# Second attention mixes two query tiles per pass, its result stored turned and normed in the projection, with stores and gate weights moved across stages

## What is computed

```python
attn = mla_attention(...)      # 4 heads of 128 value columns, causal softmax over 2048 keys
lru  = rg_lru_branch(...)      # 512 columns
mixed = concat([rms_norm(attn, attn_out_norm), rms_norm(lru, lru_out_norm)])
x  = x + gate1 * (mixed @ w_out)
h2 = rms_norm(x, norm2_g) * (1 + scale2) + shift2
x  = x + gate2 * hierarchical_moe(h2, ...)    # 32 experts, 2 for each row
```

## Time and profile before

| | us |
|---|---|
| median of 3 runs | 4110.98 (4110.75 to 4111.8) |
| the profiled execution, its own time | 4112.5 |
| span of its instructions | 4110.2 |
| busy in the span: TensorE, VectorE, ScalarE, POOL | 3780.2, 1954.9, 1557.4, 545.3 |

### The profile page before, as it was taken

One profiled execution on the slowest core, in us unless ns is written; L12 is line 12 of the kernel. 1 busy time (PEld: TensorE's weight loads), 2 busy tenths in 40 slices (PEclk: granted clock), 3 DMA queues, 4 the chain that ended last, 5 costly groups with the idle time before them and its releaser, 6 DMA issues. The chain is left out here.

```text
span 4110.2 us, 63078 instructions
## 1 busy us (share of the span) xinstructions
PE 3780.2 (92%) x21816; PEld 2452.9 (60%) x21834; DVE 1954.9 (48%) x4191; ACT 1557.4 (38%) x3427; POOL 545.3 (13%) x748
## 2 busy tenths in 40 slices
PE   6999999799889976999999799996999899599998
PEld 4667666555674534777777677773666555344444
DVE  1344333566575552111111278876333344678886
ACT  1122212356553431111111266664333222267675
POOL 0000000100260000111111001101000000322222
PEclk8999999899999988999999899997999999699999
DMA  6221121222524476656656212215221133488974
GB/s 237 77 89 70 68 97 56 86 85 79 162 87 177 163 275 249 209 171 206 203 164 217 69 49 66 67 37 151 62 89 45 42 124 125 179 292 297 318 244 102
DMA packets 228193, 573.83 MB, mean 140 GB/s; under 512 B 28170, under 2 KB 103051, under 8 KB 212159
## 3 DMA queue, kind: packets, MB, share of 16 engines
q1 hardware_dynamic: 178782, 395.92, 27.5%
q0 software_dynamic: 49248, 175.79, 14.5%
HBM read 433.59 MB, written 137.93 MB: 139 GB/s over the span
## 5 line engine op out<-in xcount | busy, mean ns | idle before, releaser
L2177 PE MATMUL out_psO<-out_w,out_mixT 128*128 128x512 f32 x1024 | 451.8, 600 | 3.0 <-ACT out_mixT L2148 1.6
L880 PE MATMUL inp_psU<-inp_w,inp_hT 128*128 128x512 f32 (+3 forms) x1376 | 420.8, 464 | 0.0
L880 PEld LDWEIGHTS inp_psU<-inp_w,inp_hT 128*128 128x128 f32 x1376 | 256.4, 190 | 152.3 <-issue 122.3
L2177 PEld LDWEIGHTS out_psO<-out_w,out_mixT 128*128 128x128 f32 x1024 | 194.0, 192 | 236.6 <-issue 236.5
L4200 DVE COPY moe_bu<-moe_wu 128x1024 f32 x480 | 299.1, 697 | 40.4 <-issue 18.2
L4087 PE MATMUL moe_psU<-moe_wu,moe_xT 128*32 x1280 | 293.4, 383 | 1.7 <-DVE moe_bu L4200 1.7
L4087 PE MATMUL moe_psU<-moe_bu,moe_xT 128*32 128x256 f32 x3840 | 294.5, 383 | 0.0
L876 PE MATMUL inp_psU<-inp_hT,inp_w 128*128 128x256 f32 x1088 | 244.4, 385 | 9.0 <-DVE inp_tm L682 4.5
L2721 PE MATMUL moe_psG<-moe_xT,moe_g_w 128*128 128x256 f32 x1024 | 234.3, 383 | 10.9 <-DMA moe_u_w<-in_w_up 10.9
L2762 ACT ACTIVATE moe_sg<-moe_psG 128x256 f32<-128x256 f32 x64 | 24.5, 383 | 577.6 <-PE moe_psG L2721 577.6
L2782 DVE TENSOR_TENSOR moe_hT<-moe_sg,moe_psG 128x256 f32<-128x256 f32 x64 | 26.9, 421 | 443.5 <-ACT moe_sg L2762 443.5
(11 more groups left out here) (687 smaller groups left out, 6700.6 us busy)
## 6 DMA issues: line engine op xcount, KB each, us to landing
moe_wu<-in_w_up SPq DMA_DIRECT2D x32, 2048.0 KB, 9.5
moe_d_w<-in_w_down SPq DMA_DIRECT2D x16, 2048.0 KB, 10.5
moe_wd<-in_w_down SPq DMA_DIRECT2D x32, 1024.0 KB, 11.3
moe_g_w<-in_w_gate SPq DMA_DIRECT2D x15, 2048.0 KB, 8.6
moe_u_w<-in_w_up SPq DMA_DIRECT2D x15, 2048.0 KB, 13.5
mod_w<-in_w_ada SPq DMA_DIRECT2D x24, 1024.0 KB, 14.1
inp_mod_w<-in_w_mod SPq DMA_DIRECT2D x16, 1024.0 KB, 4.9
xn<-out_xn POOLq DMA_DIRECT2D x32, 512.0 KB, 3.8
```

What stands on the lines that cost most here:

```text
L880: mm = pe.matmul(psU[:, u % NB, 0:n], hT[:, par, k, j * P:(j + 1) * P], w[:, k, lo:lo + n], start=(k == 0), stop=(k == KD - 1))
L2177: mm = pe.matmul(psO[:, j, h, :], mixT[:, j, k, :], out_weights.half[k // 4][:, k % 4, h * BANK:(h + 1) * BANK], start=(k == 0), stop=(k = ...
```

## The change

- In the second attention, two neighbouring query tiles (0 and 1, 2 and 3, ...) form a pair. `mix` now has a value block stationary and the probabilities of both tiles moving, 256 columns, and sums into one PSUM tile of 256 columns; a key block that only the odd tile sees moves 128 columns. So the result is made turned (value columns by queries). `pT` now holds all key blocks of a pair, once for long and once for short tiles. Which parts are mixed in which unit is worked out ahead (`mixed_by`); at most units one part (two key blocks), after the unit's `turn`.
- The engine that copies the unit's probabilities also copies a finished pair from PSUM to `o`. The reciprocals of the sums (`invert`) go by POOL to DRAM as one row of 256 numbers, and back spread over 128 partitions; VectorE multiplies `o` by them (`divide`), and POOL stores the pair turned.
- The second projection norms the turned attention: squares, a sum over four blocks, one matmul by ones that sums over the partitions and spreads the sum (`sum_squares`, between the two halves of `product`), square root on ScalarE, reciprocal and four products on VectorE. The four transposes and the copy are gone in block 2.
- In both projections the half of tiles 0 and 1 that needs no norm is multiplied first (`direct_part`). SP's first loads are in a new order, and x, gate row and router weights come last.
- The window attention, the recurrence and the second attention no longer wait for their last stores; the projection's SP does, before it reads them (`LeavingRows`).
- In `choose_rows` SP loads expert 0's gate weights and stores the chosen rows ahead of the modulation. In `experts` only halves of up are loaded for expert 0, the gate row comes after expert 0's loads, and POOL's first gather waits for the first half of up.
- The first half of the output weights, the turned input of the second projection and two buffers of the second experts move into one shared buffer with these gate weights.

```diff
 class SharedRows:
+        self.weights = nc.alloc_sbuf_tensor("shared_weights", [P, 4 * D], F32)
+        self.gate_landed = nc.alloc_semaphore("first_expert_gate_landed")
+    def load_gate(self, sp, w_gate):
+        sp.dma_start(self.weights_of(KD, FF1), w_gate[0:1, :, :].rearrange("e (k p) n -> p (e k) n", p=P)).then_inc(self.gate_landed, 16)
...
 def mlstm (and window_attention, latent_attention):
-            for x in range(2):
-                pool.wait_ge(stored[x], 16 * (NC - SKIP))
...
 def out_projection, sync:
-                rows.load_first(sp, 0)
+                direct_rows.all_stored(sp)
+                rows.load_direct(sp, 0, 0)
+                mix_rows.all_stored(sp)
+                rows.load_mix(sp, 0, 0)
+                rows.load_direct(sp, 1, 1)
+                sp.dma_start(nw[:, :], rows.norm_w.to_broadcast([P, 512])).then_inc(nw_landed, 16)
+                rows.load_mix(sp, 1, 1)
             out_weights.load_rest(sp)
-                rows.load_first(sp, 1)
+                for t in range(2):
+                    rows.load_x(sp, t, t)
...
 vector:
+            def norm_turned(t, j):
+                ch.done(dve.tensor_tensor(sq[:, 0:512], hv, hv, ALU.mult))
+                dve.tensor_reduce(sqs[:, :], sq[:, 0:512].rearrange("p (k t) -> p t k", k=4), AX, ALU.add).then_inc(msq, 1)
+                dve.wait_ge(rooted, t + 1)
+                ch.done(dve.reciprocal(root[:, :], root[:, :]))
+                for k in range(4):
+                    ins = dve.scalar_tensor_tensor(out=mixT[:, j, k, :], in0=mix[:, j, k * P:(k + 1) * P], scalar=nw[:, k:k + 1],
+                                                   in1=root[:, :], op0=ALU.mult, op1=ALU.mult)
...
 tensor:
+            def direct_part(t):
+                for h in range(2):
+                    for k in range(rows.direct, rows.direct + 4):
+                        pe.matmul(psO[:, t, h, :], mixT[:, t, k, :], out_weights.half[k // 4][:, k % 4, h * BANK:(h + 1) * BANK],
+                                  start=(k == rows.direct), stop=False)
...
+                ks = range(normed, normed + 4) if early(t) else range(KD)
                 for h in range(2):
+                    if h and layer == 2 and there(t + 1):
+                        sum_squares(t + 1)
+                    for k in ks:
...
+            def sum_squares(t):
+                pe.wait_ge(msq, t + 1)
+                pe.matmul(psM[:, 0:P], K["ones"][:, :], sqs[:, :], start=True, stop=True).then_inc(turned, 1)
...
 def choose_rows, sync:
-            mod.put(sp)
+            shared.load_gate(sp, w_gate)
             sp.wait_ge(rows_ready, 1)
...
+            mod.put(sp)
...
 def latent_attention, tensor:
-                for c in range(4 * g, min(4 * g + 4, tile_of[n] + 1)):
-                    mm = pe.matmul(psO[:, n % 2, :], pT[:, u % 2, c % 4, :], v[h % 2][:, c, :],
-                                   start=(c == 0), stop=(c == tile_of[n]))
+                    if x:
+                        pe.wait_ge(*out_count(x - 1))
+                pe.wait_ge(*kept_count(n, q // 2))
+                for c in (2 * q, 2 * q + 1):
+                    if c <= top:
+                        mm = pe.matmul(psO[:, :], v[h % 2][:, c, :], pT[k][:, c, :, :].rearrange("p x t -> p (x t)"),
+                                       start=(c == 0), stop=False)
+                    else:
+                        mm = pe.matmul(psO[:, P:2 * P], v[h % 2][:, c, :], pT[k][:, c, 1, :], start=False, stop=True)
...
 keep:
+            if parts_before(n, g):
+                wait(mixed, parts_before(n, g))
...
+            for x in range(NP):
+                if last_unit[x] == u:
+                    wait(mixed, first_part[x + 1])
+                    if x >= 2:
+                        wait(*stored_count(x - 2))
+                    copy(o[:, x % 2, :], psO[:, :]).then_inc(out_kept[keeper[x]], 1)
...
 vector:
+            def divide(x):
+                dve.wait_ge(*out_count(x))
+                dve.wait_ge(rb_landed, 16 * (x + 1))
+                dve.tensor_tensor(o[:, x % 2, :], o[:, x % 2, :], rb[:, x % 2, :], ALU.mult).then_inc(o_ready, 1)
...
 gpsimd:
+            for x in range(NP):
+                pool.wait_ge(rch, ends[x] + 1)
+                pool.dma_start(r_rows[x:x + 1, :].rearrange("a (j p) -> p (a j)", p=P), rc[:, x % 4, :], allow_slow_non_contiguous=True
+                               ).then_inc(r_stored, 16)
+                pool.wait_ge(r_stored, 16 * (x + 1))
+                pool.dma_start(rb[:, x % 2, :], r_rows[x:x + 1, :].to_broadcast([P, 2 * P])).then_inc(rb_landed, 16)
+                if x:
+                    put(x - 1)
```

More of the change, by code:

```diff
@@ L1038, in load_first, with __init__, all_stored @@
             sp.dma_start(self.wr[:, :, :], self.w_router).then_inc(self.wr_landed, 16)
+class LeavingRows:
+    def __init__(self, nc, stack, name, width, stores):
+        self.tile = stack.enter_context(nc.sbuf_tensor(f"{name}_o", [P, 2, width], F32))
+        self.stored = [nc.alloc_semaphore(f"{name}_stored{j}") for j in range(2)]
+        self.ALL = 16 * stores
+    def all_stored(self, engine):
+        for j in range(2):
+            engine.wait_ge(self.stored[j], self.ALL)
 class SharedRows:
@@ L1196, in _ @@
             blocks(pool, put)
-            for j in range(2):
-                pool.wait_ge(stored[j], 16 * (NBLK // 2))
         @block.tensor
@@ L2219, in body @@
                     product(n + 1, 1 - j)
-                if there(n + 2):
+                if there(n + 2) and layer == 1:
                     turn(n + 2, j)
@@ L2227, in body @@
                     route(n - 1)
+            for t in range(2):
+                direct_part(t)
+                if t == 0 and layer == 2:
+                    sum_squares(0)
             steps(pe, body)
@@ L2645, in _ @@
                 load(0, j, True)
+                if scatter and j == 0:
+                    sp.dma_start(gr[:, :], gate_row.to_broadcast([P, D])).then_inc(fixed, 16)
             with sp.Fori(1, TURNS) as i:
@@ L3567, in latent_attention, with parts_before @@
     unit_of = [(n, g) for n in range(N) for g in range(groups[n])]
+    UNITS = len(unit_of)
+    ends = [n for n in range(N) if sum(kind[m] == kind[n] for m in range(n)) % 2]
+    NP = len(ends)
+    pair_of = [ends.index(n) if n in ends else min(x for x, e in enumerate(ends) if e > n and kind[e] == kind[n]) for n in range(N)]
+    low_tile = [tile_of[e] // 2 * 2 for e in ends]
+    parts = [low // 2 + 1 for low in low_tile]
+    first_part = [sum(parts[:x]) for x in range(NP + 1)]
+    part_of = [(x, q) for x in range(NP) for q in range(parts[x])]
+    ready_at = [first_group[ends[x]] + q // 2 for x, q in part_of]
+    before = [max([y for y in range(x) if kind[ends[y]] == kind[ends[x]]], default=-1) for x in range(NP)]
+    def parts_before(n, g):
+        y = before[pair_of[n]]
+        return first_part[y] + min(2 * g + 2, parts[y]) if y >= 0 else 0
+    mixed_by, made = [], 0
+    for u in range(UNITS):
+        ready = sum(r < u for r in ready_at)
+        made = max(min(made + 1, ready), parts_before(*unit_of[u]))
+        assert made <= ready or made == 0
+        mixed_by.append(made)
+    mixed_by[-1] = len(part_of)
+    last_unit = [min(u for u in range(UNITS) if mixed_by[u] >= first_part[x + 1]) for x in range(NP)]
+    last_tile = [unit_of[u][0] for u in last_unit]
+    keeper = [kind[n] for n in last_tile]
     with Stage(nc, "lata") as s:
@@ L3675, in _ @@
                     turn(n, g)
[L3676 to L3677 removed]
+                    while done < mixed_by[first_group[n] + g]:
+                        mix(*part_of[done])
+                        done += 1
                     if g == 0:
@@ L3725, in _ @@
                     bound(n + 2)
-            divide(N - 1)
+                while divided < NP and last_tile[divided] < n:
+                    divide(divided)
+                    divided += 1
+            while divided < NP:
+                divide(divided)
+                divided += 1
         @block.scalar
```

250 lines of the change are left out of this document (143 added, 107 removed).

## The result

The changed kernel takes 4128.98 us (median of 5 runs, 4126.42 to 4134.88) against 4110.75 us before, ratio 1.0047 with a 95% interval of 1.0032 to 1.0061. It is slower by some 18 us, where 47 us less were forecast. The span of the profiled execution is 4125.2 us; it was 4110.2. The two traces thus stand 15.0 us apart; the other 3 us of the medians are in no trace.

What follows compares the result with a forecast made beforehand. TensorE was taken to bound the second attention, busy 402.1 of 417.1 us. Gains of 24.4 - 6 + 5.4 + 8.7 + 1 + 13.9 = 47.4 us took 4110.98 to 4063.6 us, range 4048 to 4084.

Steps and rivals of the forecast that it cites:

- Part 1: Second attention: mixing two query tiles at once, 0.458 us per wide matmul against 0.276 per narrow, gains 24.4 us.
- Part 2, the detour costed at nothing: Second attention: sums' trip through DRAM, a 6.2 us chain, hides in a pair's 12.5 us and costs nothing.
- the nearer row: Sums' store priced like an unloaded 4 KB vector load in 4-byte pieces, which landed in 2.8 us.
- The far end: Sums' store priced like a vector load behind other loads, 7.8 us, making the detour's chain 16.7 us.
- rival C: Second attention: the sums' detour sets the pace; at 16.7 us a pair the stage takes 534 us, total 4199; chance 0.03.
- Part 2, the waits: Second attention: TensorE's waits grow from 14.2 to 20 us, 6 us lost (4 gained to 16 lost).
- 26 units get no mixing: Second attention: by walking the schedule, 26 of 160 units lack mixing to fill TensorE's waits, the first six included.
- Part 3: Second output projection: earlier start, cheaper tiles and a loss near the end together gain 5.4 us (1 to 9).
- Start: Second output projection: multiplying halves that need no norm first starts the third product 3.0 us earlier.
- Tiles: Second output projection: one ones-matmul replacing four transposes saves 0.3 us on each of 13 tiles, 3.9 us.
- Picks: Near the second output projection's end, VectorE also picks experts: a new 3.1 us wait, counted as 1.5 us lost.
- Parts 4 and 5: First output projection and recurrence gain 8.7 us, window attention 1; choosing rows and first experts gain 13.9.

Runs made afterwards that it cites:

- old_att: The changed kernel with the second attention and the second projection's norm and transposes as before, all other edits kept; 4084.7 us, ratio 0.9939.
- the ring: The changed kernel without the sums' detour (division left out), its turned long probabilities' buffer enlarged from 16 to 24 blocks, used as six groups in rotation; 4111.6 us.
- sp_sums: The changed kernel with both DMAs of the sums issued on SP's queue, POOL storing only the results; 4153.5 us.
- wide_sums: The changed kernel with the reciprocal sums stored as 128 pieces of 8 bytes instead of 256 of 4; 4116.7 us.

## Why the prediction was wrong

**Part 1, the step that failed first.** "One matmul of the program is two records: 544 matmuls of 0.276 us" divided the busy time of a group by its count. The groups are short, mostly two to eight records between transposes, and each one's busy time has a tail of some 0.16 us that lies under the next group. The wide price came from a stage with groups of 16 records, where the same tail weighs little, so the two prices were not alike. From start to start a narrow matmul takes 0.22 us and a wide one 0.44: 544 x 0.22 = 119.7 against 256 x 0.44 + 32 x 0.22 = 119.7. Summed over every record of both traces, from its start to the next start without idle time, mixing takes 125.3 us before and 126.0 after. The forecast gain of 24.4 us was 2 or 3 at most. The lower bound of 0 was the right value, but the range never held it: its "parts 1 and 2 give 8 to 28" takes part 2's bounds alone. The check was at hand: 544 x 128 columns are 256 x 256 and 32 x 128.

**Part 2, the detour costed at nothing.** I took 2.8 us for a store of 256 pieces, from the nearer row, a load of 4 KB in an unloaded stretch; it is a store, and lands in 9.7 (8.4 to 16.2). The far end, 7.8, was the better guide; the 2 us per DMA that the prediction also tried is further off, for no such store landed in under 8.4. In the middle the slack of 12.5 us a pair all but covers it (5.1 us lost, at most 1.9 of them in waits), so rival C's price was not reached, but POOL was close to it: 28 times of 32 the sums lay ready when it came to them. At the end that queue shows. The last reciprocals were there 12 us ahead of the last mixing, little less than store and load take from issue to landing (9.7 and 4.7), but POOL issued their store behind it, so store, load, product and store all stood there: 14.4 us in the gap. That an earlier issue would have hidden most of them is worked out from these rows and was not run. I looked for what hides the detour, not at where the one engine that carries it, pair after pair, would stand when the loop ends.

**Part 2, the waits.** Forecast 20 us against 14.2; measured 25.6 without the sums, 27.5 with them (sums of the waits view). The kinds were right, long exponentials and turned tiles; the exponentials were mis-sized, 11.7 and not 6. 11.4 more than before, with 2.6 more of busy time (404.7 against 402.1) and a gap shorter by 2.3, make the 11.8 us that are no matter of the sums. Against old_att, whose same old attention ran 3.5 us faster, they would be 15.3. That "26 units get no mixing" is the cause was argued; the ring shows that the buffer is not, and the pace moved little, so the cause of the longer waits stays open. I also wrote that two accumulators became one. The old code waits for the previous division ahead of every tile, both halves lying in one bank, so there was one before as well.

**Part 3.** Start: gain forecast 3.0, measured 2.0 (third product 35.4 us after the stage's start against 37.4). Tiles: from 16.48 to 16.26 us (mean of tiles 3 to 11), 2.8 in 13 tiles against 3.9. Picks: forecast 1.5 lost, measured 5, the wait of 3.4 and 1.3 for the eight records behind it, at the lower granted clock. Net nothing, where 5.4 were forecast: my reading that "VectorE is the later engine there" was what failed, for its lateness was a wait for logits that a reordering takes away.

**Parts 4 and 5 were right.** By the lengths of the stages in both traces: first projection 7.7 us (7.0 forecast), recurrence 1.8 (1.7), choosing rows 4.5 (4.8), window attention 0.35 (1), experts and the stage behind them 9.1 (9.1), with the first expert product 7.0 us after its stage starts, exactly where it was put. That is 23.5 of 23.6. The traces stand 20.6 apart there, because the changed execution was already 2.9 us late ahead of the first edit. That is no chance of one execution: the window attention's first matmul starts at 782.7 us in before and at 784.4 to 786.1 in all nine kernels with the new attention, though at 779.7 in old_att; the cause is open. Counted from the window attention's start, old_att gains 25.7.

The sum then reads: 20.6 gained ahead of the attention (23.6 forecast), 34.5 lost in it (18.4 gained forecast, parts 1 and 2), 1.1 lost behind it: 15.0, the difference of the spans.

## What to carry to other kernels

Price an instruction by the distance from its start to the next start, in a row of the order of time, and never by busy time over count where groups are short; here matmuls with the same columns cost the same to 2% however they were cut. For a detour over DRAM that fits into the period of a loop, ask when the last turn's data is ready and when the issuing engine gets to it: here 12.8 us later, which put the whole detour behind the loop. Before a scattered store is accepted, lay its source so that its pieces grow: here that alone gave back 10 of 18 us. And before a few microseconds of a stretch are put down to an edit, look at the granted clock in it.

## What the runs showed of the hardware

A store of 1 KB in 256 pieces of 4 bytes lands in 9.7 us (median of 32), in 128 pieces of 8 bytes in 3.9, and beside the first kind the stores of 128 KB took 4.8 us and not 2.2. Issued by SP right behind the seven loads of a head, the next DMA held SP for about 15 us: the scattered store of sp_sums for 14.9 and 15.5 us, the loads of the output weights of before for 15.2. After a pause of 3.4 us eight records of 512 columns took 3.60 us in one place (granted clock 1.00) and 4.88 in another (0.50); in wide_sums, behind the same two pauses, 6.08 and 5.30. After a pause of 2.36 us the same records ran at 0.50 in one execution and at 1.00 in another. So the same pause may or may not cost the clock.
